# Fifteen more words in a four-byte tile ahead of the late arena of a one-core decoder layer

## The reference, cut to what matters

```python
h = rms_norm(x, g_mix);  z = h @ w_in                      # 1024 x 7168
q, k, v, u, gate_a, gate_s = split(z)
a = dilated_attention(q, k, v, g_q, g_k) @ w_attn_proj     # 3 dilation groups x 8 heads x 64
y = gelu(s5_ssm(u, ...));  s = (y @ w_glu_a) * sigmoid(y @ w_glu_b)
x = x + (sigmoid(gate_a) * a + sigmoid(gate_s) * s) @ w_out
h2 = rms_norm(x, g_ffn)
x = x + (silu(h2 @ w_ffn_gate) * (h2 @ w_ffn_up)) @ w_ffn_down   # inner width 2816
```

## Time and profile before

| | us |
|---|---|
| median of three runs | 902.76 |
| the profiled execution's own time | 902.23 |
| its span, first to last instruction | 900.4 |
| TensorE matmul busy | 882.5 (98% of the span) |
| VectorE / ScalarE / GpSimd busy | 447.9 / 326.2 / 189.8 |
| TensorE clock granted, mean | 1.000 |

### The profile page before, as it was taken

One profiled execution on the slowest core, in us unless ns is written; L12 is line 12 of the kernel. 1 busy time (PEld: TensorE's weight loads), 2 busy tenths in 40 slices (PEclk: granted clock), 3 DMA queues, 4 the chain that ended last, 5 costly groups with the idle time before them and its releaser, 6 DMA issues.

```text
span 900.4 us, 12851 instructions
## 1 busy us (share of the span) xinstructions
PE 882.5 (98%) x4472; PEld 720.8 (80%) x4472; DVE 447.9 (50%) x625; ACT 326.2 (36%) x487; POOL 189.8 (21%) x219
## 2 busy tenths in 40 slices
PE   5999999999999999999999999999999999999998
PEld 4887888888897887877887888888888888788886
DVE  5554775677914543543577554333333334433334
ACT  5312343323236656756423333222222222223321
POOL 4699988930020000001220220000000000000000
PEclk9999999999999999999999999999999999999999
DMA  7429334584464552412225232333333232222212
GB/s 274 139 86 240 96 117 140 160 185 140 134 161 153 181 158 71 130 68 73 94 88 184 79 111 79 94 95 95 95 95 97 95 94 93 100 95 93 93 70 94
DMA packets 84705, 106.67 MB, mean 118 GB/s; under 512 B 10528, under 2 KB 51664, under 8 KB 84544
## 3 DMA queue, kind: packets, MB, share of 16 engines
q1 hardware_dynamic: 80096, 96.34, 34.0%
q0 software_dynamic: 1408, 3.61, 2.3%
q10 hardware_dynamic: 3168, 6.29, 2.0%
HBM read 92.29 MB, written 13.93 MB: 118 GB/s over the span
## 4 chain that ended last, share of the span: by engine, by line
PE 52%; DVE 2%; issue 1%; ACT 0%; DVEq 0%; ACTq 0%
PE ps L1408 27%; PE ps L1438 12%; PE ps L1167 12%; DVE late L1149 1%; PE ps L1376 0%; DVE late L1069 0%; DVE hT_lo L1075 0%; PE ps L1313 0%; PE ps L1299 0%; DVE w_lo L550 0%; ACT w_hi L544 0%; PE ps L1423 0%; DVE late L1113 0%; DVE late L1072 0%; PE ps L1418 0%
## 5 line engine op out<-in xcount | busy, mean ns | idle before, releaser
L550 DVE TENSOR_TENSOR w_lo<-w_raw,w_hi 128x1024 fp32r<-128x1024 f32 x142 | 200.7, 1414 | 342.4 <-ACT w_hi L544 342.4
L544 ACT ACTIVATE w_hi<-w_raw 128x1024 fp32r<-128x1024 f32 x142 | 150.4, 1059 | 408.6 <-PE ps L1167 164.0
L1408 PE MATMUL ps<-h_hi,w_hi 128*128 128x512 f32 x352 | 139.4, 396 | 0.0
L1408 PE MATMUL ps<-h_hi,w_lo 128*128 128x512 f32 x352 | 139.2, 395 | 0.0
L1408 PE MATMUL ps<-h_lo,w_hi 128*128 128x512 f32 x352 | 139.2, 395 | 0.0
L401 POOL TENSOR_TENSOR early<-early 128x16 f32<-128x16 f32 (+8 forms) x141 | 128.3, 910 | 23.3 <-ACT early L567 12.4
L1167 PE MATMUL ps<-w_hi,hT_hi 128*128 128x512 f32 x288 | 114.1, 396 | 12.0 <-DVE w_lo L550 11.9
L1167 PE MATMUL ps<-w_hi,hT_lo 128*128 128x512 f32 x288 | 113.1, 393 | 0.0
L1167 PE MATMUL ps<-w_lo,hT_hi 128*128 128x512 f32 x288 | 113.1, 393 | 0.0
L1167 PE MATMUL ps<-hT_hi,w_hi 128*128 128x512 f32 x224 | 91.6, 409 | 0.0
L1167 PE MATMUL ps<-hT_hi,w_lo 128*128 128x512 f32 x224 | 87.6, 391 | 0.0
(11 more groups left out here) (197 smaller groups left out, 1076.9 us busy)
## 6 DMA issues: line engine op xcount, KB each, us to landing
w_raw<-in_w_in SPq DMA_DIRECT2D x112, 256.0 KB, 3.3
w_raw<-in_w_ffn_gate SPq DMA_DIRECT2D x44, 256.0 KB, 2.8
w_raw<-in_w_ffn_up SPq DMA_DIRECT2D x44, 256.0 KB, 3.0
w_raw<-in_w_ffn_down SPq DMA_DIRECT2D x44, 256.0 KB, 2.7
z_d<-early ACTq DMA_DIRECT2D x6, 1024.0 KB, 4.8
late<-z_d SPq DMA_DIRECT2D x96, 64.0 KB
w_raw<-in_w_out SPq DMA_DIRECT2D x16, 256.0 KB, 3.0
z_d<-early SPq DMA_DIRECT2D x3, 1024.0 KB, 6.7
```

Of the source, the lines that this page charges most:

```text
L544: nc.scalar.activation(w_hi[:, j % WSPL], w_raw[:, j % WRAW], ACT.Copy).then_inc(w_hi_done, 1)
L550: nc.vector.tensor_tensor(w_lo[:, j % WSPL], w_raw[:, j % WRAW], w_hi[:, j % WSPL].bitcast(F32), ALU.subtract).then_inc(w_lo_done, 1)
L1408: ins = T.matmul(ps[:, m], (w_hi, w_lo)[b][:, j % WSPL, at_w:at_w + P], (h2_hi, h2_lo)[a][:, 2 * j + h, :], start=j == 0 and h == 0 and k ...
```

## The change

`minus_half` gets 16 words instead of one. Its values, and the one word that is read, stay as they are. The tile takes 64 bytes where it took 32 (4, rounded up), and all tiles behind it in the list move up by 32 bytes: `ones` and `norm_row` from 64 to 96 past a multiple of 128, `norm_all`, `early`, `yT`, `o_sum`, `aT`, `late` and `h2` from 96 past to a multiple of 128. The memset of line 411 writes 16 columns instead of one.

```diff
-        minus_half = sb(ctx, "minus_half", [P, 1])
+        minus_half = sb(ctx, "minus_half", [P, 16])
         ones = sb(ctx, "ones", [P, P])
         norm_row = sb(ctx, "norm_row", [P, TB])
         norm_all = sb(ctx, "norm_all", [P, SEQ])
```

## The result

The changed kernel takes 890.32 us (median of 4 runs, 889.83 to 890.90) where the kernel before takes 902.85 us (4 runs): ratio 0.9859, 95% interval 0.9842 to 0.9876. It is 12.5 us faster.

A forecast was written before the change was run, and what follows sets the result against it. TensorE's rate through ready matmuls was taken as the bound. 8.96 us from large matmuls less 0.32 given back made 8.64, so 902.76 became 894.1 us; the 8-in-10 range was 891.3 to 896.0 us.

The forecast's parts named there:

- The DMAs: Loads into SBUF: first ones might land 0.4 us sooner, only the start waits; taken as 0, 0.4 us either side.
- The large matmuls: 1344 matmuls of `ffn`, `yT` and `aT` go from 233.3 to 226.7 ns if spacing follows the moving operand's address: 8.96 us.
- What hides or gives back: All matmul savings reach the end, except at the gated mix near 479 us, where TensorE waits longer: 0.32 us lost.
- The small matmuls, `ones`: Attention and state-space matmuls taken as 0, at most 2.8 us; 32 matmuls on `ones` and `norm_row` 0, at most 0.2 us.
- VectorE: VectorE's remainders and products take the same time aligned or unaligned, so no effect was expected.
- The place: Rival: matmul spacing follows where in memory operands lie, not alignment, so moving 32 bytes does nothing: 902.8 us, chance 0.10.
- A larger multiple: Rival: large matmuls need a larger alignment unit, so only half of 8.64 us is gained: 898.4 us, chance 0.05.
- The small matmuls: Rival: attention and state-space matmuls gain as well, 2.8 us more, 11.4 us in all: 891.3 us, chance 0.05.
- The clock: Rival: denser feed-forward matmuls draw TensorE's clock to its lower level, with a tenth of `ffn` slowed: 915 us, chance 0.03.

The follow-up runs named there:

- uc_only: Kernel before, with 8 spare words ahead of `uc`, so `uc` begins on a multiple of 256 while `h2`, `yT`, `aT` stay unaligned: 900.21 us, ratio 0.9966.
- late_only: Kernel before, with 32 bytes allocated between `early` and the late tiles, so only `yT`, `o_sum`, `aT`, `late`, `h2` become aligned: 894.20 us, ratio 0.9899.
- h2_16b: Changed kernel, with `h2_hi` and `h2_lo` begun 16 bytes further on, 144 past a multiple of 256, weights at 128: 895.64 us, ratio 0.9919.

## Why the prediction was wrong

*The step that failed is "The DMAs".* I compared loads of 2 KB rows into `w_raw` with loads of 4 KB rows into `early` and found 6%, bounded that at 0.4 us and wrote that only the start waits for the loads. Three things were missing. The rows looked at were long ones; the gathers move 256-byte pieces, and off a multiple of 256 they landed in 5.3 to 7.1 us, on one in 4.0 to 4.7. The DMA view had their 6.3 us for 128 KB, twice the time of a weight load for half its size. And something did wait for them: by the code, a weight load stands in the same queue behind them, and the waits list had ScalarE waiting up to 3.2 us for `w_raw`, after the start. Measured, this term is 3.1 us (2.0 to 4.2) in `uc_only`, and 8.64 + 3.1 = 11.7 us would have given 891.0. The 0.7 us that are left are within the interval of either part.

The Trainium skill has a rule on this that I passed over: "DMA: Bandwidth & Descriptors", section "How a descriptor splits into AXI transactions", says that transactions begin at multiples of 256 bytes. From this I work out that a 256-byte piece off such a start needs two. The page speaks of reads; here the pieces are written to `uc`. The table above agrees with it in that, 4.0 to 4.7 us at 0 and 5.3 to 7.1 elsewhere, though no run counts the transactions.

*The large matmuls* had the right size for the wrong reason, which is luck. All 1344 went to 226.7 ns, and `late_only` shows 9.1 us (7.9 to 10.5) for this part, with 8.64 predicted. But I said that the spacing goes with the moving operand alone, by its own alignment. That the stationary operand is `w_hi` or `w_lo` at 233.3 ns and at 226.6 shows that the weights are not the cause by themselves; it doesn't exclude that the two positions count together. In the trace of before the two readings can't be told apart, as all operands at 226.7 ns had equal positions. The change put `h2` where the weights are, by chance of the 128 bytes; with `[P, 48]`, which is aligned better, 2.3 us would have been left of 12.5.

*What hides or gives back* was right at the mix (0.31 us of 0.32). From 413 to 479 us 0.98 us came and not 1.44: TensorE also waited 0.25 us more at the starts of two weight tiles (near 415 and 457 us), which I had put at nothing, and the other 0.2 us are spread over the stretch. *The small matmuls, `ones`:* nothing, as taken. *VectorE:* its remainders have no address effect, but they wait for GpSimd's products, and I had not looked at when they begin.

*The rivals.* The place: refuted by the change. A larger multiple: not as I meant it; 256 matters, but as the modulus of a difference. The small matmuls: no part. The clock: granted at 1.00 in all stretches of `ffn`. The Trainium skill's lines of 16 bytes ("SBUF — State Buffer", section "Door 1: The DMA port swizzle") predict no cost for `h2_16b`, whose operands both begin on multiples of 16; it is 5.0 ns for each matmul, so the measurement decides against that reading.

What stays open: why the positions of the two operands meet in this way. TensorE reads the next stationary operand while it streams the moving one (weight loads are busy for 81% of the span and matmuls for 98%, so they run side by side), and a conflict between these two reads is a natural guess, but no run here separates it from others.

## What to carry to other kernels

Where matmuls stream back to back, read their spacing by operand, and put the tiles that a matmul reads together at equal addresses modulo 256 bytes; a constant spacing a few per cent above another one for the same shape is the sign. This is shown for float32r matmuls with 128x128 stationary and 512 moving columns, and for no other form. Start the target of a DMA with 256-byte pieces on a multiple of 256. And before writing that no one waits for a transfer, follow the queue it stands in: the load behind it may be what an engine waits for.

## What the runs showed of the hardware that I had not expected

The spacing of 512-column float32r matmuls depends on the difference of two addresses modulo 256: 226.7 ns at 0, 231.7 at 16 bytes, 233.3 at 32, 228.9 at 64, 233.3 at 96, 232.4 at 128. It neither rises nor falls all along. Eight gathers of 128 KB, 2.3 us quicker each, were worth 3 us of the whole. A VectorE remainder that began during a GpSimd product ended 1.08 to 1.11 us after that product's end, whenever it had begun, and so took between 1.2 and 5.4 us; the late weight tile moved two of them to where they took 8.63 us together.
